# A two-block network kernel: the first block's queues written in another order, and its state inputs taken two at a time

## The reference, cut to what matters

```python
u = rmsnorm(h, norm_mix)
u_ssm, q, k, v = split(u @ w_in)                      # 512 columns each
# state branch: 32 groups of 16 channels, 64 complex states each
bu = u_ssm (per group) times b_bar                    # real and imaginary part
x_t = a_bar * x_{t-1} + bu_t                          # along the 256 tokens
y = Re(C x) + D_skip * u_ssm;  y = gelu(y)
y_ssm = y * sigmoid(y @ w_glu + b_glu)
# attention branch: 8 heads of 64, stick-breaking weights, s < t only
z = q k^T / 8;  y_attn = exp(log_sigmoid(z) + suffix sums of log_sigmoid(-z)) @ v
merged = sigmoid(gate) * (y_ssm @ w_up_ssm) + sigmoid(gate) * (y_attn @ w_up_attn)
h = h + merged @ w_out                                # then the MLP of block one, then block two
```

## Time and profile before

| what | value |
|---|---|
| median of 3 runs | 1611.33 us (1610.52 to 1612.16) |
| the profiled execution | 1610.34 us |
| its span, first to last instruction | 1608.1 us |
| TensorE busy | 1566.7 us, 97% |
| VectorE busy | 1100.3 us, 68% |
| ScalarE busy | 834.8 us, 52% |
| granted TensorE clock, mean | 0.993 of full |

### The profile page before, as it was taken

How to read it: one execution, slowest core, us unless ns; L and a number is a source line. 1 busy time by engine, 2 the same in 40 slices (tenths; PEclk the granted TensorE clock), 3 DMA queues, 4 the chain that set the end, 5 groups by cost and what they waited for, 6 DMA issues and landing times.

```text
span 1608.1 us, 24651 instructions
## 1 busy us (share of the span) xinstructions
PE 1566.7 (97%) x9702; PEld 1357.8 (84%) x9702; DVE 1100.3 (68%) x1466; ACT 834.8 (52%) x1104; POOL 25.7 (2%) x46
## 2 busy tenths in 40 slices
PE   8999899999999999999999999999999999999997
PEld 8887878888788889887978888888889888888886
DVE  7988676666756578777675657765677776676566
ACT  7768553344544356656454435544455566454443
POOL 1002000000000000000000000000000000000001
PEclk9999999999999999999999999999999999999998
DMA  8432435557455665533455565456564525446652
GB/s 245 130 104 79 150 126 183 186 193 237 146 195 180 198 197 141 172 106 106 158 167 172 183 206 188 155 184 207 183 202 139 175 63 153 161 132 194 197 183 105
DMA packets 206875, 264.52 MB, mean 164 GB/s; under 512 B 14170, under 2 KB 176340, under 8 KB 206804
## 3 DMA queue, kind: packets, MB, share of 16 engines
q1 hardware_dynamic: 206612, 263.50, 51.2%
q10 hardware_dynamic: 192, 0.04, 0.0%
HBM read 262.47 MB, written 1.05 MB: 164 GB/s over the span
## 4 chain that ended last, share of the span: by engine, by line
PE 88%; DVE 8%; ACT 3%; issue 1%; DMA 0%; ACTq 0%; DVEq 0%
PE bank L452 44%; PE bank L486 22%; PE bank L490 11%; DVE wl L419 3%; PE bank L1828 1%; ACT wh L412 1%; PE bank L1225 1%; DVE wl L438 1%; PE bank L1842 1%; DVE norm_small L749 1%; PE bank L697 1%; PE bank L1238 1%; PE bank L1857 1%; PE bank L830 1%; PE bank L1951 0%
## 5 line engine op out<-in xcount | busy, mean ns | idle before, releaser
L419 DVE TENSOR_TENSOR wl<-raw,wh 128x2048 fp32r<-128x2048 f32 (+2 forms) x228 | 509.6, 2240 | 99.1 <-ACT wh L412 96.0
L412 ACT CAST wh<-raw 128x2048 fp32r<-128x2048 f32 (+3 forms) x235 | 437.2, 1865 | 89.7 <-PE bank L452 89.1
L486 PE MATMUL bank<-u_parts,wh 128*128 128x512 f32 x1664 | 424.2, 392 | 1.5 <-DVE u_parts L793 1.0
L486 PEld LDWEIGHTS bank<-u_parts,wh 128*128 128x128 f32 x1664 | 302.9, 188 | 59.7 <-issue 2.0
L452 PE MATMUL bank<-u_parts,wh 128*128 128x256 f32 (+1 forms) x1344 | 253.8, 289 | 2.8 <-DVE u_parts L793 2.0
L490 PEld LDWEIGHTS bank<-u_parts,wl 128*128 128x128 f32 x1664 | 231.2, 190 | 15.4
L490 PE MATMUL bank<-u_parts,wl 128*128 128x256 f32 x1664 | 243.0, 282 | 0.0
L452 PEld LDWEIGHTS bank<-u_parts,wh 128*128 128x128 f32 (+1 forms) x1344 | 208.6, 190 | 8.7 <-issue 4.7
L452 PE MATMUL bank<-u_parts,wl 128*128 128x256 f32 (+1 forms) x672 | 190.3, 283 | 0.0
L452 PE MATMUL bank<-wh,hh 128*128 128x512 f32 x448 | 178.8, 399 | 7.1 <-DVE wl L419 5.1
L452 PE MATMUL bank<-wl,hh 128*128 128x512 f32 x448 | 174.9, 390 | 0.0
(11 more groups left out here) (340 smaller groups left out, 1963.8 us busy)
## 6 DMA issues: line engine op xcount, KB each, us to landing
raw<-ffn_wg SPq DMA_DIRECT2D x44, 1024.0 KB, 5.8
raw<-ffn_wu SPq DMA_DIRECT2D x44, 1024.0 KB, 5.3
raw<-ffn_wd SPq DMA_DIRECT2D x44, 1024.0 KB, 5.0
raw<-w_ff SPq DMA_DIRECT2D x32, 1024.0 KB, 5.3
raw<-w_in SPq DMA_DIRECT2D x28, 1024.0 KB, 5.5
raw<-w_out SPq DMA_DIRECT2D x12, 1024.0 KB, 5.0
raw<-w_gate SPq DMA_DIRECT2D x8, 1024.0 KB, 5.6
raw<-w_in SPq DMA_DIRECT2D x16, 512.0 KB, 5.3
```

The source lines that it names most:

```text
L412: ins = act.copy(dst, src)
L419: ins = dve.tensor_tensor(dst, src, upper.bitcast(F32), ALU.subtract)
L486: return pe.matmul(two(bank[b + f]), slab_view(wh, slot, KD, WCOLS)[:, k, f * P:(f + 1) * P], u_parts[:, k, :, :], start=k == 0, stop=Fals ...
```

## The change

No step is added or taken away on TensorE, and the weights and the results stay. Four things are different:

1. `pe_bu` is called with two states. Its loop then issues the real parts of both, and the imaginary parts of both: matmuls that follow each other stand on different 32 partitions and write different banks. There are 8 such calls where there were 16. A call waits until both banks were read.
2. The places of all small steps between the slabs differ on the three engines: when heads are started, summed and weighted, where splits and roundings stand.
3. GELU, its rounding and rest, and the product with the sigmoid, its rounding and rest are done in two halves of two tiles each. The two matmuls behind them wait per half.
4. ScalarE rounds slab `N_GLU` ahead of the last two heads' weights, and slab `N_UP1 + 3` ahead of the sigmoid. VectorE takes the rest of GELU ahead of the split of `N_UP1 + 2`.

The core of the diff:

```diff
-            pe_bu(pe, 0)
+            pe_bu(pe, 0, 1)
...
-            pe_bu(pe, 2)
+            pe_bu(pe, 2, 3)
...
-            pe.wait_ge(gelu_l, 1)
             pe.wait_ge(w_exp, HEADS)
-            lin_pe(pe, N_GLU, 2, None, KS, DS, 4, *upper(0))
+            lin_pe(pe, N_GLU, 2, lambda k: pe.wait_ge(gelu_l, k // 2 + 1), KS, DS, 4, *upper(0))
...
-            pe.wait_ge(glu_l, 1)
-            lin_pe(pe, N_UP1 + 3, 2, None, KS, 512, 4, *upper(0))
+            lin_pe(pe, N_UP1 + 3, 2, lambda k: pe.wait_ge(glu_l, k // 2 + 1), KS, 512, 4, *upper(0))
...
             act.wait_ge(y_taken, 4)
-            link(act.activation(us[:, :, :], us[:, :, :], ACT.Gelu_apprx_tanh))
-            act.copy(bh[:, 0:KS, :], us[:, :, :]).then_inc(gelu_h, 1)
+            for i in range(2):
+                link(act.activation(us[:, 2 * i:2 * i + 2, :], us[:, 2 * i:2 * i + 2, :], ACT.Gelu_apprx_tanh))
+                act.copy(bh[:, 2 * i:2 * i + 2, :], us[:, 2 * i:2 * i + 2, :]).then_inc(gelu_h, 1)
             act_round(act, N_UP1 + 2)
+            act_round(act, N_UP1 + 3)
             wait_used(act, N_GLU)
...
             dve_split(dve, N_GLU)
+            for i in range(2):
+                dve.wait_ge(gelu_h, i + 1)
+                dve.tensor_tensor(bl[:, 2 * i:2 * i + 2, :], us[:, 2 * i:2 * i + 2, :], bh[:, 2 * i:2 * i + 2, :].bitcast(F32),
+                                  ALU.subtract).then_inc(gelu_l, 1)
             dve_split(dve, N_UP1 + 2)
             for b in range(2):
                 dve.wait_ge(lin_free[b], 8)
-            dve.wait_ge(gelu_h, 1)
-            dve.tensor_tensor(bl[:, 0:KS, :], us[:, :, :], bh[:, 0:KS, :].bitcast(F32), ALU.subtract).then_inc(gelu_l, 1)
```

More of the change, by code:

```diff
@@ L1371, in b1_pe @@
             pe_slab1(pe, 4, 0)
[L1372 removed]
+            pe_bu(pe, 0, 1)
             pe_slab1(pe, 4, 1)
             b1_pe_vec2(pe)
[L1375 to L1378 removed]
+            pe_slab1(pe, 5)
+            pe_bu(pe, 2, 3)
             pe_z(pe, 0)
             pe_slab1(pe, 6, 0)
[L1381 removed]
+            pe_z(pe, 1)
             pe_slab1(pe, 6, 1)
[L1383 to L1384 removed]
+            pe_slab1(pe, 7)
+            pe_bu(pe, 4, 5)
             pe_tri(pe, 0)
[L1386 removed]
             pe_y(pe, 0)
+            pe_y(pe, 2)
+            pe_z(pe, 2)
+            pe_slab1(pe, 8)
             pe_av(pe, 0)
[L1389 to L1390 removed]
+            pe_tri(pe, 1)
             pe_slab1(pe, 9, 0)
[L1392 to L1394 removed]
+            pe_z(pe, 3)
+            pe_bu(pe, 6, 7)
+            pe_tri(pe, 2)
+            pe_av(pe, 1)
             pe_slab1(pe, 9, 1)
[L1396 to L1398 removed]
             pe_slab1(pe, 10, 0)
[L1400 removed]
+            pe_bu(pe, 8, 9)
+            pe_slab1(pe, 10, 1)
             pe_y(pe, 4)
[L1402 to L1404 removed]
+            pe_z(pe, 4)
+            pe_y(pe, 6)
+            pe_tri(pe, 3)
             pe_slab1(pe, 11, 0)
[L1406 to L1419 removed]
+            pe_tri(pe, 4)
+            pe_av(pe, 2)
+            pe_bu(pe, 10, 11)
+            pe_av(pe, 3)
+            pe_z(pe, 5)
+            pe_slab1(pe, 11, 1)
+            pe_slab1(pe, 12)
             pe_slab1(pe, 13, 0)
@@ L1427, in b1_pe @@
             pe_y(pe, 10)
-            pe_av(pe, 4)
             pe_slab1(pe, 14, 1)
-            pe_bu(pe, 14)
+            pe_tri(pe, 6)
+            pe_av(pe, 5)
+            pe_bu(pe, 14, 15)
             pe_z(pe, 7)
-            pe_av(pe, 5)
-            pe_tri(pe, 6)
+            pe_y(pe, 12)
             pe_slab1(pe, 15, 0)
-            pe_bu(pe, 15)
-            pe_y(pe, 12)
             pe_av(pe, 6)
@@ L1572, in b1_act @@
             act_softplus(act, 0)
+            act_softplus(act, 1)
             act_evict(act, 6)
+            act_evict(act, 7)
+            act_weights(act, 0)
             act_round(act, 9)
-            act_weights(act, 0)
-            act_softplus(act, 1)
-            act_evict(act, 7)
             act_round(act, 10)
-            act_turns(act, 2)
-            act_round(act, 11)
+            act_softplus(act, 2)
             act_evict(act, 8)
             act_weights(act, 1)
+            act_turns(act, 2)
+            act_softplus(act, 3)
+            act_round(act, 11)
+            act_o(act, 0)
+            act_phase(act, 2)
+            act_weights(act, 2)
             act_round(act, 12)
             act_evict(act, 9)
[L1585 to L1588, removed]
+            act_softplus(act, 4)
+            act_evict(act, 10)
+            act_turns(act, 3)
+            act_weights(act, 3)
+            act_weights(act, 4)
+            act_o(act, 1)
             act_round(act, 13)
-            act_softplus(act, 3)
-            act_evict(act, 10)
+            act_softplus(act, 5)
+            act_evict(act, 11)
+            act_phase(act, 3)
             act_round(act, 14)
[L1593 to L1596, removed]
             act_round(act, 15)
             act_evict(act, 12)
[L1599 to L1602, removed]
+            act_evict(act, 13)
+            act_round(act, N_UP1)
             act_softplus(act, 6)
             act_weights(act, 5)
-            act_evict(act, 13)
-            act_round(act, N_UP1)
             act_o(act, 2)
@@ L1610, in b1_act @@
             act_evict(act, 14)
+            act_round(act, N_GLU)
             act_weights(act, 7)
@@ L1623, in b1_act @@
                                      bias=v1("b_glu")(f))
[L1624 to L1627, removed]
+                if f % 2:
+                    ins.then_inc(glu_sig, 1)
+            for i in range(2):
+                act.wait_ge(glu_y, i + 1)
+                act.copy(bh[:, 2 * i:2 * i + 2, :], us[:, 2 * i:2 * i + 2, :]).then_inc(glu_h, 1)
             act_round(act, N_UP1 + 4)
@@ L1660, in b1_dve @@
             dve_split(dve, 7)
+            dve_split(dve, 8)
             dve_state(dve, 2)
[L1662 removed]
             dve_state(dve, 3)
```

60 lines of the change are left out of this document (32 added, 28 removed).

## The result

The changed kernel takes 1594.68 us (median of 4 runs, 1592.69 to 1595.29) beside 1610.92 us for the kernel before on the same chip (4 runs, 1610.42 to 1612.16). The medians are 16.2 us apart, where 14.6 were forecast. The ratio on record is 0.9894 with a 95% interval of 0.9879 to 0.9909, 1.06% faster (the two medians by themselves give 0.9899). The ratio, taken from the 1611.33 us of the prediction, gives 1594.2 us: 2.5 us under the forecast of 1596.7 and 0.3 us under the low end of its range, 1594.5. The median as measured, 1594.68, lies 2.0 us under the forecast.

The account below looks back on a forecast made before the run. TensorE was taken to bound the kernel; 8.5 (pairs) + 0.7 (shapes) + 4.1 (GELU wait) + 1.3 (clock) = 14.6 us, new places 0, so 1611.33 - 14.6 gives 1596.7 us. Own range 1594.5 to 1599, overall 1594.5 to 1602.5.

Parts of the forecast that it names:

- can only cost: New places of small steps between the slabs on all queues: cost 0, bounded by 5 us; no gain expected from them.
- The bound: TensorE, 88% of the last-ending chain; gains only from fewer microseconds of its rows and the 3.9 us wait.
- The input pairs: State inputs between the slabs: two states in 1.06 us, what one cost before; 8.5 us saved over eight pairs.
- the row of the same kind of group: Block two's trace at 713.25: two heads on separate 64 partitions, 0.86 us measured where full overlap gives 0.85.
- partial-overlap rival: State inputs: only inner passes pair, 6 passes, 1.49 us a pair; saves 5.0 not 8.5, 1600.2 us; chance 0.12.
- Fewer changes of shape: TensorE returns to slab or sum rows 17 times, not 21, at 0.19 each: 0.7 us, bounds 0 and 1.3.
- The GELU wait and the clock: Gated unit: waits of 3.9 and 0.2 us for the rests go, 4.1 us; clock drop behind goes, 1.3 us.
- thin margins: TensorE's slack in the new order: 0.5 to 1.6 us at some pairs, sums, head steps and N_UP1; no wait forecast.
- The low end of the range: Whole kernel: 1594.5 us, from a pair at 0.93 us and all 1.3 us of the changes of shape.
- No overlap: State inputs: a pair still costs 2.12 us, giving 1605.2 us; chance 0.05.
- New waits for VectorE: VectorE's load rises to 95%, a few margins fail, TensorE waits 3 to 6 us: 1599.7 to 1602.7; chance 0.14.
- Slower: Seven pair calls from 2+3 on wait at TensorE's queue head for the second bank: about 1629 us; chance 0.03.

Follow-up runs that it names:

- sums_apart: Changed kernel with head 2's scores moved between the sums pe_y(0) and pe_y(2), which stood together; 1595.26 us, a single run.
- states_parted: Changed kernel with every pair of state inputs taken apart, the second state 24 slab rows later, all else as changed; 1605.52 us, ratio 0.9954.
- not_in_turn: Changed kernel with each pair written as two single pe_bu calls one right behind the other, places kept; 1595.71 us, ratio 0.9899.
- tail_only: Kernel before with only the gated unit changed: halves, rest of GELU ahead of the split, roundings earlier; 1605.59 us, ratio 0.9963.
- split_first: Changed kernel with VectorE's split of N_UP1 + 2 put ahead of the rests of GELU again, halves kept; 1597.58 us, a single run.
- pairs_only: Kernel before with only the state inputs by twos, each pair at its first state's place; 1617.38 us, ratio 1.0041.
- tail_undone: Changed kernel with the gated unit as before: one piece, old order of roundings and splits; 1601.75 us, ratio 0.9943.
- sums_by_four: Changed kernel with sums of states 0 to 3 and 4 to 7 taken four in turn, head 4's scores moved ahead; 1592.67 us, ratio 0.9880.

## Why the prediction's sum was wrong, and what in it held

**The step that failed.** The prediction says of the new places "These can only cost", puts them at 0, and walks every `pe_y` at 1.85 us, wherever it stands. But the new places put `pe_y(0)` and `pe_y(2)` next to each other, and there their rows overlap in part: 2.75 us for both instead of 3.70. The new places gained 0.95 us by this. Sums_apart measured it by parting the two (0.94 us), and states_parted, with the new places and the states apart, has the same 2.75 us in its chain. I had the two in adjacent lines of the diff, and the earlier trace rows show alternating column groups overlapping inside one call; I asked what stands on separate parts of the array inside a call and not what stands so across two. A second term was too small: the wait for GELU and the clock behind it, 5.4 us, measured 5.8 (below). A third part of the difference, 0.3 us at the start, is luck.

**The bound.** Right. TensorE had all of the touched stretch, its rows and its waits were the two places to gain, and states_parted shows the pace follows its rows one to one.

**The input pairs, 8.5 us.** Right to the digit: 1.06 us for two states at every one of the eight places, and 8.5 us back when they are parted. The price from the row of the same kind of group held, and the partial overlap did not occur. The Trainium skill, "TensorE: Matmul & The Clock Gate", section "Measured speedup vs the span model", gives 3.07 times for four row groups, from which I had estimated 1.38 us a pair; for two groups the trace, with 1.06, doesn't agree with such a loss. The mechanism behind it was told too narrowly. The partial-overlap rival (6 passes, 1.49) supposed that the order within the pair matters, and so did my expectation of not_in_turn. It doesn't matter.

**Fewer changes of shape, 0.7 us.** Right in size. The slab phase is the time from the first state to the first row of `N_UP1`. That row in the kernel before, and in the changed one:

```profile
167.16 0.39 PE L452 MATMUL bank<-bh,wh 128*128 128x256 f32 x1
```

```profile
156.71 0.39 PE L452 MATMUL bank<-bh,wh 128*128 128x256 f32 x1
```

In the timeline the first state starts at 44.05 and at 43.77, so the phase shrank from 123.1 to 112.9 us, by 10.2. With 8.5 for the pairs and 0.95 for the sums, 0.7 are left for the changes of shape; states_parted, which takes four of them back, gives 0.6.

**The GELU wait and the clock, 4.1 + 1.3 us.** Right in place and mechanism (tail_only, split_first), and short in size: from the start of `N_UP1` to the MLP the two kernels take 63.16 and 57.32 us, 5.8 apart and not 5.4. Some 0.3 of it is in how a wait is read. An idle time counts from the end of the last row, but rows that follow each other start every 0.12 us and are 0.28 long. The last row before the gap, in TensorE's timeline of the kernel before, and the first behind it:

```profile
172.89 0.28 PE L452 MATMUL bank<-bh,wl 128*128 128x256 f32 x1
177.08 0.58 PE L452 MATMUL bank<-bh,wh 128*128 128x256 f32 x1 [3.91 <-DVE bl L1699]
```

From start to start these are 4.19 us for a step of 0.12: the gap cost 4.07, not 3.91, and the short one behind it 0.16 more in the same way. The clock gave back 1.4 to 1.5 us and not 1.3 in this execution. That GELU's halves were wanted for it, as the working had it, was wrong: with the whole GELU nothing waits either.

**The new places as a danger.** None of the thin margins failed, as forecast. But pairs_only, with the old places, is slower than the kernel before: the new places made a loss of 3.3 us at the MLP into a gain, and "can only cost" was wrong in this respect too.

**The start.** The first state came 0.28 us earlier (43.84 for 44.12), and no edit decides it. In the kernel before, as in tail_undone and sums_apart, TensorE's clock is low for a while at 15 to 20 us; in the changed kernel, tail_only and split_first it isn't. The window of sums_apart, then that of the changed kernel:

```profile
15.00:20.00 5.00, 5.00 (x31) 5.00 (x31) 4.79 (x14) 4.41 (x6) 0.00 (x0) 0.66 1.10 183
```

```profile
15.00:20.00 5.00, 5.00 (x42) 5.00 (x43) 4.77 (x14) 4.42 (x6) 0.00 (x0) 1.00 1.08 180
```

31 rows or 42 in the same 5 us, 1.3 us at 0.12 a row. tail_only has the full clock there though its first 150 us are the old ones, and tail_undone the low one though they are the new. What does differ is TensorE's idling just ahead, in the norm in front of the slabs. The kernel before:

```profile
PE bank L452 <- DVE u_parts L793: 2.0, 1, 2.0
```

It is 1.9 to 2.5 us in the seven kernels that show the low clock, and 1.3 in four of the five that don't (the changed one among them); the fifth, split_first, has 1.9 and kept the full clock, so that wait alone does not settle it. Most of the 1.3 us is lost again to the 0.8 us wait for a split; only 0.3 us of it reaches the first state.

**The arithmetic of the whole.** Start 0.3, pairs 8.5, changes of shape 0.7, adjacent sums 0.95, gated unit 5.8: 16.3 us at the MLP, and 16.2 by the medians. The profiled spans differ by 15.0 only, since this execution of the changed kernel has one drop of the clock more, at 390 to 395 us (0.67; the kernel before reads 1.00 at the same place, for it 405 to 410 us):

```profile
390.00:395.00 5.00, 5.00 (x16) 3.92 (x16) 4.23 (x8) 0.14 (x1) 0.00 (x0) 0.67 0.48 150
```

The low end of the range was built wrong as well. The two bounds that the prediction names for it, a pair at 0.93 and 1.3 us for the changes of shape, save 16.2 us with the other terms, which is 1595.1 and not the 1594.5 that it states. Neither number had room for a gain that stood in no term.

**The rivals.** No overlap and partial overlap: refuted by the 1.06 us. New waits for VectorE: none in the changed kernel, but sums_by_four, which takes 2.7 us more out of TensorE's queue, meets them, so the warning was for a kernel one step further on. Slower: its mechanism is real, and pairs_only shows it; the new places are what keeps it away.

## What to carry to other kernels

In this kernel, float32 matmuls on separate rows or separate columns of the array ran side by side when they stood next to each other in the queue, whichever call wrote them; so look in a diff for small steps that have become neighbours, and price them together. A call that wants two results at once waits for the later one with all of the queue behind it: move it to where both are there, and count the moving as part of the gain. When a queue is cut that close to the next engine's load, walk that engine forward before taking out more.

## What the runs showed of the hardware

- **Overlap across calls.** Two groups of 32 partitions that write different banks: 8 rows in 1.06 us, in turn or one state behind the other (1.07), where the second state's rows start together with the first's. Two pairs of 32-column groups one behind the other: 2.75 us for 3.70. Four column groups in turn: 32 rows in 1.86 us.
- **The clock behind a gap is not one price.** Gaps of 3.9 us in front of the same 48 rows cost 1.5 us of clock in the kernel before, 2.8 in pairs_only and 2.9 in tail_undone. Behind the gap of 2.0 us in split_first the clock stayed at full.
- **Drops come and go between kernels at places that no edit touched.** At 15 to 20 us the window reads 0.66 or 1.00, and in the changed kernel 0.67 at 390 to 395 us where the kernel before reads 1.00. Each is 1.3 us or so of slow rows. Ahead of the second place TensorE has idled for 2.02 us, up to 389.01 us in the changed kernel:

```profile
389.01 0.47 PE L452 MATMUL bank<-wh,hh 128*128 128x512 f32 x1 [2.02 <-issue]
```

  All twelve kernels have this gap of 2.02 us in their traces (the kernel before up to 405.30), and five of them show a drop behind it. What decides stays open.
